# One 64-column matmul in place of two 32-column ones beside two other 32-column matmuls

## The chip, the cores and the metric

The kernel runs on one core of a Trainium2 chip. The metric is device time in microseconds (us), the median of three runs. All times below are of that core.

## The reference

A stack of two transformer layers is followed by a third block with attention, spatial gating, a cross attention and a mixture of experts, all in fp32 on 512 tokens of width 1024. The change touches the mixture of experts alone. Each token is routed to 2 of 16 experts; the reference computes all of them and weighs them:

```python
for e in range(N_EXPERTS):
    he = jax.nn.silu(t @ w_gate[e]) * (t @ w_up[e])
    y = y + combine[:, e:e + 1] * (he @ w_down[e])
```

with t of 512x1024, w_gate and w_up of 1024x512 and w_down of 512x1024 for each expert.

## The kernel before

The kernel sorts the experts by the number of tokens that chose them, and gathers their tokens into tiles of at most 128 rows. A popular expert has a tile to itself. Experts with few tokens share one: `SHARED` names, for a tile, triples (place of the expert in the sorted order, first row, rows). Tile 0 holds two experts of 64 rows each. Tile 1 holds four experts of 32 rows. Tile 2 holds places 6 and 7 with 32 rows each and place 8 with 64 rows, which is written as two parts of 32 rows. `GROUPS` is the order of the tiles: 0, 2, (8 and 10), 7, (9 and 11), 6, 5, 4, 3, 1. For each, `fan` computes the gate and up products (1024 deep, 512 wide, into two PSUM banks), and `fold` the down product (512 deep, 1024 wide). The fan of a tile runs ahead of the fold of the one before it: fan 0, fold 0, fan 2, fan (8, 10), fold 2, fan 7, fold (8, 10), and so on.

For a shared tile the gathered rows are the stationary operand, in plain fp32, and the expert's weights stream from their buffers (`RAW`, and `ST` or `X` where a buffer of another stage is reused) as they come from HBM. Each part of the tile is a matmul of its own: 128 rows deep, as many columns wide as the part has rows, 512 elements streamed, with its output on the PSUM partitions that start at the part's first row. `fan_shared` goes through 8 steps of k for each of gate and up, 16 in all, and `fold_shared` through 4 steps for each of two halves, 8 in all. I call one of these 24 a step; it issues one matmul call for each part (the inner loop over `SHARED[i]`). The profile shows every fp32 call as two MATMUL records, each with a weight load of its own. Other tiles use weights split into two parts (`WH`, `WL`) by ScalarE and VectorE and three matmuls with all 128 columns.

Each weight buffer is 512 KB. SyncE's queue loads them in a fixed order; a load waits until the tile that had its buffer 24 loads before was used (key `wf`, raised by the last matmul that reads it, or `lo`, raised when it was split). Which instruction comes when on each engine is fixed at build time by a planner (`lay_out`) that keeps a clock of its own for each engine. A shared tile's matmul call costs it 856 / (number of parts) ns, so a step costs 856 ns there whatever the number of parts.

GpSimd gathers the rows of a tile (`XG`) and adds a tile's results into `sum` in DRAM by indirect transfers (`sum<-EY,PUT`), one after the other.

Of the kernel before, what the change touches and what calls it, by code (L numbers as in the profile page):

```python
# [343 lines left out]
def build(nc, A, out):  # L344
# [133 lines left out]
    G, S, TP, OP = Ring(ps[0:3]), Ring(ps[3:5]), Ring(ps[5:7]), Ring(ps[7:8])  # L478
# [23 lines left out]
    def view(ap, kind):  # L502
        if kind == "A":
            return ap.rearrange("p (a c) -> p a c", a=4)
        if kind == "B":
            return ap.rearrange("p (a c) -> p a c", a=2)
        return ap.rearrange("p (a s c) -> p a s c", a=2, s=2)
# [7 lines left out]
    def tile_k(w, k, n):  # L515


        if n == 512:
            return w.rearrange("(p k) c -> p k c", k=8)[:, k:k + 2, :], "B"
        return w.rearrange("(p k) (s c) -> p k s c", k=4, s=2)[:, k, :, :], "B"  # L520
# [35 lines left out]
    def cols(T, n=128):  # L556
# [5 lines left out]


    SHARED = {0: ((0, 0, 64), (1, 64, 64)), 1: ((2, 0, 32), (3, 32, 32), (4, 64, 32), (5, 96, 32)),
              2: ((6, 0, 32), (7, 32, 32), (8, 64, 32), (8, 96, 32))}
    PLACES = {i: sorted({p for p, _, _ in parts}) for i, parts in SHARED.items()}
    GROUPS = ((0,), (2,), (8, 10), (7,), (9, 11), (6,), (5,), (4,), (3,), (1,))
    SLOTS = sum(GROUPS, ())
    LAST = SLOTS[-1]
# [6 lines left out]
    def tensor(pe):  # L576
        pe.c = 0

        def tile(src, kind, use="split"):
            c = pe.c  # L580
            pe.c += 1
            if c == len(TILES):
                TILES.append((src, kind, use))
                split = sum(w is not None for w in WAT[MARKS["few"]:]) if "few" in MARKS else None
                WAT.append(None if use == "whole" else c % 8 if split is None else split % 4)
            if use == "whole":
                return c, None, None
            k = kind if kind == "A" else "B"
            return c, view(WH[:, WAT[c], :], k), view(WL[:, WAT[c], :], k)

        def whole_tile(c):
            return view(RAW[RAWSLOT[c] if c < len(RAWSLOT) else 0][:, :], "B")
# [183 lines left out]
        def weight(place, name, k, use):  # L776


            if place < 2:
                return tile(*tile_k(A[name][0, 15 - place], k, 1024 if name == "w_down_2" else 512), use)  # L780
            return tile((name, k, 16 + place if place < 16 else place - 15), "B", use)
# [4 lines left out]
        def fan(gr):  # L786

            if gr[0] in SHARED:
                yield from fan_shared(gr[0])
                return  # L790
            for k in range(8):
                if k % 2 == 0:
                    tiles = [split_weight(gr, name, k) for name in ("w_gate_2", "w_up_2")]
                done = lambda i, c: [("wf", c)] if i == gr[-1] and k % 2 else []
                for i in gr:
                    if small(i):
                        pe.wait_ge(*(yield [("ex", i, 0), *[("raw", c) for c, _, _ in tiles],
                                            G.ask(("fan", i)) if k == 0 else None]))
                        ex, o = pe.slot("ex", i)[1], pe.slot("fan", i)
                        for g, (c, _, _) in enumerate(tiles):  # L800
                            t = pe.mm(o[64 * g:64 * g + 64, :], ex[:, k, 0:64], whole_tile(c)[:, k % 2, :], k == 0, k == 7, 445)
                        keys = done(i, tiles[0][0]) + done(i, tiles[1][0]) + ([("fan", i), ("free", ("ex", i))] if k == 7 else [])
                        if keys:
                            t.then_inc(*pe.sig("pe_gemm", *keys))
                        continue
                    for g, (c, wh, wl) in enumerate(tiles):
                        pe.wait_ge(*(yield [("ex", i, k // 4), ("lo", c), G.ask(("fan", i, g)) if k == 0 else None]))
                        ex, o = pe.slot("ex", i)[0], pe.slot("fan", i, g)
                        pe.mm(o[:, :], ex[:, k, :], wh[:, k % 2, :], k == 0, False)
                        pe.mm(o[:, :], ex[:, k, :], wl[:, k % 2, :], False, False)  # L810
                        t = pe.mm(o[:, :], ex[:, 8 + k, :], wh[:, k % 2, :], False, k == 7)
                        keys = done(i, c) + ([("fan", i, g)] if k == 7 else []) + (
                            [("free", ("ex", i))] if k == 7 and g else [])
                        if keys:
                            t.then_inc(*pe.sig("pe_gemm", *keys))

        def fan_shared(i):

            for k in range(0, 8, 2):
                tiles = [{p: weight(p, name, k, "whole")[0] for p in PLACES[i]} for name in ("w_gate_2", "w_up_2")]  # L820
                for g in range(2):
                    pe.wait_ge(*(yield [("ex", i, k // 4), *[("raw", c) for c in tiles[g].values()],
                                        G.ask(("fan", i, g)) if k == 0 else None]))
                    ex, o = pe.slot("ex", i)[1], pe.slot("fan", i, g)
                    for h in range(2):
                        for p, r, n in SHARED[i]:
                            t = pe.mm(o[r:r + n, :], ex[:, k + h, r:r + n], whole_tile(tiles[g][p])[:, h, :], k + h == 0,
                                      k + h == 7, 856 / len(SHARED[i]))
                            last = r + n == 128 or p != SHARED[i][-1][0]
                            end = k + h == 7 and r + n == 128  # L830
                            keys = ([("wf", tiles[g][p])] if h and last else []) + ([("fan", i, g)] if end else []) + (
                                [("free", ("ex", i))] if end and g else [])
                            if keys:
                                t.then_inc(*pe.sig("pe_gemm", *keys))
# [28 lines left out]

        def fold_shared(i):
            for k in range(4):
                tiles = {p: weight(p, "w_down_2", k, "whole")[0] for p in PLACES[i]}
                for nh in range(2):
                    pe.wait_ge(*(yield [("eh", i), *[("raw", c) for c in tiles.values()],
                                        S.ask(("fold", i, nh)) if k == 0 else None]))
                    eh, o = pe.slot("eh", i)[1], pe.slot("fold", i, nh)  # L870
                    for p, r, n in SHARED[i]:
                        t = pe.mm(o[r:r + n, :], eh[:, k, r:r + n], whole_tile(tiles[p])[:, nh, :], k == 0, k == 3,
                                  856 / len(SHARED[i]))
                        last = r + n == 128 or p != SHARED[i][-1][0]
                        end = k == 3 and r + n == 128
                        keys = ([("wf", tiles[p])] if nh and last else []) + ([("fold", i, nh)] if end else []) + (
                            [("free", ("eh", i))] if end and nh else [])
                        if keys:
                            t.then_inc(*pe.sig("pe_gemm", *keys))
# [2174 lines left out]
    gemms, _, extra = tensor(lister)  # L3054
# [17 lines left out]
    for c, (src, kind, use) in enumerate(TILES):  # L3072
# [49 lines left out]
        i = c - moe  # L3122
# [14 lines left out]
    def strands(lane):  # L3137
        lane.expert, lane.real = None, not isinstance(lane.e, Dry)
        if lane.name == "T":
            _, main, extra = tensor(lane)  # L3140
            return main, extra, []
        return {"A": scalar, "V": vector, "G": pool, "S": sync}[lane.name](lane)
# [5 lines left out]
    parts = {ln.name: strands(ln) for ln in lanes}  # L3148
# [68 lines left out]
```

## Time and profile before

| | |
|---|---|
| time, median of 3 runs | 2116.9 us (2114.93 to 2122.71) |
| profiled execution, its own time | 2114.93 us |
| span in its profile | 2113.1 us |
| TensorE matmul busy | 2012.1 us, 95% |
| VectorE busy | 1264.4 us, 60% |
| ScalarE busy | 983.1 us, 47% |
| bytes moved by DMA | 337.99 MB, mean 160 GB/s |

The page counts the matmuls of parallel column groups as one stretch of busy time, since it takes the union of their records. A record of a matmul includes its way through the array, so it is longer than the distance to the next one; the distances between starts are what to read. The experts' stage covers about the last 300 us of the span. In it the DMA engines are nearly always busy.

### The profile page before, as it was taken

What the parts mean: (1) busy time and instruction counts of PE and PEld (TensorE: products, weight loads), DVE (VectorE), ACT (ScalarE), POOL (GpSimd) and SP (SyncE); (2) the same over time, 40 slices, a digit from 0 to 9 for tenths busy, and PEclk for the clock granted to TensorE, in tenths of its full rate; (3) what the DMA queues carried; (4) which work ended last, traced back from release to release, by engine and by line L of the source; (5) the groups of instructions that cost most, each with busy time, mean ns of one, the idle gap of its engine ahead of it and who ended that gap; (6) DMA issues with size and microseconds to landing.
All of it is one profiled execution on the core that took longest, in us unless ns stands there. A gap on an engine that the chain in (4) does not pass through costs nothing.

```text
span 2113.1 us, 27983 instructions
## 1 busy us (share of the span) xinstructions
PE 2012.1 (95%) x10531; PEld 1595.4 (75%) x10531; DVE 1264.4 (60%) x2204; ACT 983.1 (47%) x1630; POOL 137.0 (6%) x238
## 2 busy tenths in 40 slices
PE   8999999999999999988999999999899999899795
PEld 7877778888888877768888888878778787646462
DVE  5575856585846356665757775737753546536563
ACT  4444545455534355544544553533563234136452
POOL 0000020000001000001000002102000000111101
PEclk9999999999999999999999999999999999999897
DMA  6235244542632333312435262462425526899898
GB/s 209 74 105 156 94 140 138 195 148 88 200 120 80 95 125 122 97 57 101 138 121 179 80 219 70 132 183 81 150 71 164 153 70 229 308 403 375 257 358 313
DMA packets 193854, 337.99 MB, mean 160 GB/s; under 512 B 15878, under 2 KB 103190, under 8 KB 193712
## 3 DMA queue, kind: packets, MB, share of 16 engines
q1 hardware_dynamic: 190096, 327.09, 45.6%
q0 software_dynamic: 3616, 9.03, 1.9%
q8 instruction: 86, 1.41, 0.3%
q14 instruction: 56, 0.46, 0.1%
HBM read 307.12 MB, written 32.51 MB: 161 GB/s over the span
## 4 chain that ended last, share of the span: by engine, by line
PE 77%; DMA 8%; DVE 7%; ACT 3%; POOL 2%; issue 2%; SPq 1%; DVEq 0%; ACTq 0%; POOLq 0%
PE ps L183 72%; PE ps L186 5%; POOL SM L218 2%; DMA ST<-in_w_up_dram 1%; DMA sum<-EY,PUT 1%; DVE WL L198 1%; ACT ST L194 1%; SPq L223 1%; DMA RAW<-in_w_down_dram 1%; DVE X L208 1%; DMA XG<-hd,IDX 1%; POOL SM L215 1%; ACT WH L194 1%; DMA ed<-ST 1%; DMA ONDP<-qkd 1%
## 5 line engine op out<-in xcount | busy, mean ns | idle before, releaser
L198 DVE TENSOR_TENSOR WL<-RAW,WH 128x1024 fp32r<-128x1024 f32 x394 | 475.0, 1221 | 268.3 <-ACT WH L194 265.4
L194 ACT ACTIVATE WH<-RAW 128x1024 fp32r<-128x1024 f32 x394 | 410.5, 1055 | 320.0 <-PE ps L183 192.6
L183 PE MATMUL ps<-XH,WH 128*128 128x512 f32 (+1 forms) x880 | 324.3, 368 | 3.8 <-DVE WL L198 3.8
L183 PE MATMUL ps<-XL,WH 128*128 128x512 f32 (+1 forms) x880 | 321.7, 366 | 0.0
L183 PE MATMUL ps<-XH,WL 128*128 128x512 f32 (+1 forms) x880 | 321.5, 365 | 0.0
L183 PE MATMUL ps<-WH,XH 128*128 128x512 f32 (+1 forms) x736 | 296.8, 403 | 2.5 <-ACT ST L194 2.5
L183 PE MATMUL ps<-WH,HR 128*128 128x512 f32 x928 | 289.2, 390 | 0.0
L183 PE MATMUL ps<-WH,XL 128*128 128x512 f32 (+1 forms) x736 | 284.8, 387 | 0.0
L183 PE MATMUL ps<-WL,XH 128*128 128x512 f32 (+1 forms) x736 | 284.1, 386 | 0.0
L183 PEld LDWEIGHTS ps<-WH,HR 128*128 128x128 f32 x928 | 174.2, 188 | 36.0
L183 PEld LDWEIGHTS ps<-XH,WH 128*128 128x128 f32 x880 | 168.8, 192 | 30.4 <-DVE WL L198 4.6
L183 PEld LDWEIGHTS ps<-XH,WL 128*128 128x128 f32 x880 | 168.5, 192 | 26.0
L183 PEld LDWEIGHTS ps<-XL,WH 128*128 128x128 f32 x880 | 168.7, 192 | 25.4
L183 PE MATMUL ps<-WL,HR 128*128 128x512 f32 x464 | 180.5, 389 | 0.0
L183 PEld LDWEIGHTS ps<-WH,XH 128*128 128x128 f32 x736 | 138.8, 189 | 33.8 <-issue 6.1
L183 PEld LDWEIGHTS ps<-WH,XL 128*128 128x128 f32 x736 | 138.5, 188 | 28.8
L183 PEld LDWEIGHTS ps<-WL,XH 128*128 128x128 f32 x736 | 139.1, 189 | 23.3
L218 POOL TENSOR_TENSOR SM<-SM 128x1 f32<-128x1 f32 (+3 forms) x106 | 68.2, 644 | 820.7 <-DVE SM L1948 441.6
L194 ACT ACTIVATE FR<-ps 128x512 f32<-128x512 f32 x80 | 47.9, 598 | 147.0 <-PE ps L183 146.6
L183 PEld LDWEIGHTS ps<-WL,HR 128*128 128x128 f32 x464 | 87.1, 188 | 17.9
L198 DVE TENSOR_TENSOR HR<-HZ,HR 128x256 fp32r<-128x256 f32 (+1 forms) x92 | 65.8, 735 | 57.3 <-ACT HR L194 56.6
L183 PE MATMUL ps<-WH,EX 128*128 128x512 f32 x224 | 78.2, 410 | 9.7 <-DVE WL L198 9.0
(368 smaller groups left out, 2781.4 us busy)
## 6 DMA issues: line engine op xcount, KB each, us to landing
RAW<-in_ffn_w_dram SPq DMA_DIRECT2D x164, 512.0 KB, 4.5
RAW<-in_w_down_dram SPq DMA_DIRECT2D x63, 512.0 KB, 14.5
RAW<-in_w_gate_dram SPq DMA_DIRECT2D x61, 512.0 KB, 9.6
RAW<-in_w_up_dram SPq DMA_DIRECT2D x57, 512.0 KB, 9.6
RAW<-in_w_in_dram SPq DMA_DIRECT2D x30, 512.0 KB
RAW<-in_ev_w_in_dram SPq DMA_DIRECT2D x20, 512.0 KB
RAW<-in_ple_w_gate_dram SPq DMA_DIRECT2D x16, 512.0 KB
RAW<-in_od_w_in_dram SPq DMA_DIRECT2D x32, 256.0 KB
```

Source lines behind the costliest of these rows:

```text
L183: return self.go(ns).matmul(o, lhsT=l, rhs=x, start=st, stop=sp)
L186: return self.go(110).transpose(o, i, ident)
L194: return self.go(0.83 * n + 55.0 + (130.0 if bias is not None else 0.0) + (100.0 if acc is not None else 0.0)).activation(o, i, f, scale=s ...
L198: return self.go(1.04 * n + 68.0).tensor_tensor(o, a, b, op)
L208: return self.go(1.04 * n + 130.0).scalar_tensor_tensor(out=o, in0=a, scalar=s, in1=b, op0=op0, op1=op1)
L215: return e.tensor_scalar(o, i, s1, None, op0) if op1 is None else e.tensor_scalar(o, i, s1, s2, op0, op1)
L218: return self.go(290.0).tensor_tensor(o, a, b, op)
L223: return e.dma_start(o, i)
```

## The change

Tile 2's third and fourth part, both of expert place 8, become one part of 64 rows. The machinery that let two parts share one weight tile goes away with them: `tiles` is a list with one entry for each part again, and the keys that free a weight tile are raised by the one matmul that reads it last. The same weights are loaded in the same order into the same buffers, and the arithmetic is the same.

```diff
     SHARED = {0: ((0, 0, 64), (1, 64, 64)), 1: ((2, 0, 32), (3, 32, 32), (4, 64, 32), (5, 96, 32)),
-              2: ((6, 0, 32), (7, 32, 32), (8, 64, 32), (8, 96, 32))}
-    PLACES = {i: sorted({p for p, _, _ in parts}) for i, parts in SHARED.items()}
+              2: ((6, 0, 32), (7, 32, 32), (8, 64, 64))}
...
-                tiles = [{p: weight(p, name, k, "whole")[0] for p in PLACES[i]} for name in ("w_gate_2", "w_up_2")]
+                tiles = [[weight(p, name, k, "whole")[0] for p, _, _ in SHARED[i]] for name in ("w_gate_2", "w_up_2")]
...
-                        for p, r, n in SHARED[i]:
-                            t = pe.mm(o[r:r + n, :], ex[:, k + h, r:r + n], whole_tile(tiles[g][p])[:, h, :], k + h == 0,
-                                      k + h == 7, 856 / len(SHARED[i]))
-                            last = r + n == 128 or p != SHARED[i][-1][0]
-                            end = k + h == 7 and r + n == 128
-                            keys = ([("wf", tiles[g][p])] if h and last else []) + ([("fan", i, g)] if end else []) + (
+                        for c, (p, r, n) in zip(tiles[g], SHARED[i]):
+                            t = pe.mm(o[r:r + n, :], ex[:, k + h, r:r + n], whole_tile(c)[:, h, :], k + h == 0, k + h == 7,
+                                      856 / len(SHARED[i]))
+                            end = k + h == 7 and (p, r, n) == SHARED[i][-1]
+                            keys = ([("wf", c)] if h else []) + ([("fan", i, g)] if end else []) + (
```

`fold_shared` is changed in the same way.

## Rows read from the trace of the kernel before

**Rows 1.** The page: span, TensorE's busy time, granted clock and DMA in 40 slices.

```profile
span 2113.1 us, 27983 instructions
...
PE 2012.1 (95%) x10531; PEld 1595.4 (75%) x10531; DVE 1264.4 (60%) x2204; ACT 983.1 (47%) x1630; POOL 137.0 (6%) x238
...
PEclk9999999999999999999999999999999999999897
DMA  6235244542632333312435262462425526899898
```

**Rows 2.** Timeline of PE, end of fold 0 and fan 2: start, length, what.

```profile
1850.79 0.59 PE L183 MATMUL ps<-RAW,EG 128*64 128x512 f32 x1
...
1851.32 2.33 PE L183 MATMUL ps<-X,EF 128*32 128x512 f32 x17
...
1854.36 10.90 PE L183 MATMUL ps<-RAW,EF 128*32 128x512 f32 x99
1865.19 0.50 PE L183 MATMUL ps<-WH,EX 128*128 128x512 f32 x1
```

**Rows 3.** Timeline of PE's weight loads: fold 0 (64 columns), fan 2 (32 columns).

```profile
1847.36 0.14 PEld L183 LDWEIGHTS ps<-RAW,EG 128*64 128x64 f32 x2 [0.29 <-issue]
...
1850.36 0.14 PEld L183 LDWEIGHTS ps<-RAW,EG 128*64 128x64 f32 x1 [0.29 <-issue]
...
1851.32 0.16 PEld L183 LDWEIGHTS ps<-X,EF 128*32 128x32 f32 x8 [0.81 <-issue]
1851.78 0.13 PEld L183 LDWEIGHTS ps<-X,EF 128*32 128x32 f32 x4 [0.30 <-issue]
...
1864.22 0.13 PEld L183 LDWEIGHTS ps<-RAW,EF 128*32 128x32 f32 x4 [0.30 <-issue]
```

**Rows 4.** Timeline of PE in fan (8, 10), from 64 to 128 columns.

```profile
1874.73 0.64 PE L183 MATMUL ps<-RAW,EX 128*64 128x512 f32 x1
...
1875.21 0.59 PE L183 MATMUL ps<-RAW,EX 128*64 128x512 f32 x1
...
1875.74 0.50 PE L183 MATMUL ps<-WH,EX 128*128 128x512 f32 x1
1876.07 0.39 PE L183 MATMUL ps<-WL,EX 128*128 128x512 f32 x1
```

**Rows 5.** Timeline of PE, fold 2 (its first 16 and last 48 records).

```profile
1889.79 1.92 PE L183 MATMUL ps<-RAW,EG 128*32 128x512 f32 x16
...
1892.32 5.36 PE L183 MATMUL ps<-RAW,EG 128*32 128x512 f32 x48
1897.61 0.50 PE L183 MATMUL ps<-WH,EX 128*128 128x512 f32 x1
```

**Rows 6.** Windows of PE: length, busy (records), clock, DMA share, GB/s.

```profile
1851.30:1865.10 13.80, 13.80 (x130) 1.00 1.03 401
1889.80:1897.50 7.70, 7.70 (x69) 1.00 1.03 409
1865.10:1888.70 23.60, 22.51 (x96) 1.00 1.03 400
```

**Rows 7.** Chain of waits: issue and landing of a weight tile of fan (8, 10).

```profile
1851.97 13.99 DMA ST<-in_w_up_dram
```

**Rows 8.** Who waited for whom, SyncE's queue, 1870 to 1930: total, times, longest.

```profile
SPq L223 <- PE ps L183: 6.2, 4, 3.3
```

**Rows 9.** The same from 1930 to 2000.

```profile
SPq L223 <- PE ps L183: 32.8, 7, 13.6
SPq L223 <- DVE WL L198: 22.4, 14, 7.8
```

**Rows 10.** Who waited for whom on PE, from 1959 to the end.

```profile
PE ps L183 <- DMA RAW<-in_w_down_dram: 8.7, 3, 5.5
PE ps L183 <- DMA RAW<-in_w_gate_dram: 3.8, 1, 3.8
...
PE ps L183 <- DMA ST<-in_w_up_dram: 2.8, 1, 2.8
```

More of the change, by code:

```diff
@@ L819, in fan_shared @@
             for k in range(0, 8, 2):
-                tiles = [{p: weight(p, name, k, "whole")[0] for p in PLACES[i]} for name in ("w_gate_2", "w_up_2")]
+                tiles = [[weight(p, name, k, "whole")[0] for p, _, _ in SHARED[i]] for name in ("w_gate_2", "w_up_2")]
                 for g in range(2):
-                    pe.wait_ge(*(yield [("ex", i, k // 4), *[("raw", c) for c in tiles[g].values()],
+                    pe.wait_ge(*(yield [("ex", i, k // 4), *[("raw", c) for c in tiles[g]],
                                         G.ask(("fan", i, g)) if k == 0 else None]))
@@ L865, in fold_shared @@
             for k in range(4):
-                tiles = {p: weight(p, "w_down_2", k, "whole")[0] for p in PLACES[i]}
+                tiles = [weight(p, "w_down_2", k, "whole")[0] for p, _, _ in SHARED[i]]
                 for nh in range(2):
-                    pe.wait_ge(*(yield [("eh", i), *[("raw", c) for c in tiles.values()],
-                                        S.ask(("fold", i, nh)) if k == 0 else None]))
+                    pe.wait_ge(*(yield [("eh", i), *[("raw", c) for c in tiles], S.ask(("fold", i, nh)) if k == 0 else None]))
                     eh, o = pe.slot("eh", i)[1], pe.slot("fold", i, nh)
-                    for p, r, n in SHARED[i]:
-                        t = pe.mm(o[r:r + n, :], eh[:, k, r:r + n], whole_tile(tiles[p])[:, nh, :], k == 0, k == 3,
+                    for c, (p, r, n) in zip(tiles, SHARED[i]):
+                        t = pe.mm(o[r:r + n, :], eh[:, k, r:r + n], whole_tile(c)[:, nh, :], k == 0, k == 3,
                                   856 / len(SHARED[i]))
-                        last = r + n == 128 or p != SHARED[i][-1][0]
-                        end = k == 3 and r + n == 128
-                        keys = ([("wf", tiles[p])] if nh and last else []) + ([("fold", i, nh)] if end else []) + (
+                        end = k == 3 and (p, r, n) == SHARED[i][-1]
+                        keys = ([("wf", c)] if nh else []) + ([("fold", i, nh)] if end else []) + (
                             [("free", ("eh", i))] if end and nh else [])
```

## The prediction

> **What bounds the kernel now.** I read the page first. TensorE is busy for 95% of the span at nearly full granted clock, and the DMA engines reach eight to nine tenths only in the last eight slices, where the experts' weights are loaded [rows 1]. So the stage of the change has two candidates for its limit, and the question is which of them tile 2's matmuls sit on.
>
> Then the timeline of TensorE around tile 2. Fan 2 starts at 1851.32 and the next group's first matmul at 1865.19 [rows 2]; fold 2 runs from 1889.79 to 1897.61, with four transposes in it [rows 5]. In both stretches TensorE is busy without a gap, at clock 1.00, while DMA is at a share of 1.03 and 401 to 409 GB/s [rows 6]. DMA is saturated too, but TensorE does not wait for it there: it runs at its own pace.
>
> What that pace is the weight loads tell. In fan 2 four loads of 32 columns start together, one for each part, and the next four come one round later: from 1851.78 to 1864.22 there are 29 rounds, (1864.22 - 1851.78) / 29 = 0.429 us each [rows 3]. In fold 0, with two parts of 64 columns, a round has two loads and is as long: seven rounds from 1847.36 to 1850.36, 0.429 us [rows 3]. So the parts of a tile run side by side in the array, and a round costs what one matmul costs, however many share it. A step (one call for each part, two records to a call) is two rounds, 0.858 us. Fan 2's 16 steps are 13.7 us, fold 2's 8 are 6.9 us, as the rows show.
>
> **The change part by part.** It removes one of four calls in each of the 24 steps: 48 of 192 matmul records and as many loads. Since a round's length does not depend on the number of calls in it, this removal alone is worth nothing: two parts and four parts both give 0.429. The weight loads (0.13 to 0.14 us) lie beside the streaming, and the transfers, evacuations and semaphores are the same.
>
> What it adds is a round whose parts have unlike widths: 32, 32 and 64 columns. The trace has no such round. It does have what happens when the width changes from one stretch to the next. From the last round with 64 columns (1850.79) to the first with 32 (1851.32) it is 0.53 us, and from there to the second 0.46 (1851.78) [rows 2, 3]. In fan (8, 10), where every step of k goes from 128 columns to 64 and back, the first round of 64 is 0.48 us long (1874.73 to 1875.21), and the next to 128 columns 0.53 (1875.21 to 1875.74) [rows 4]. Two kinds of change of width, and at each the distance is about 0.10 us above the steady 0.429, with a first round behind a change that is 0.03 to 0.05 longer. The pattern of fan (8, 10) repeats in each of the eight steps of k, with everything landed, so it is not the wait for data. I read it as the array finishing what is in it before it takes another width.
>
> If that holds inside a step, the 64-column call can't run beside the 32-column ones. A step becomes: first round of places 6 and 7, second round, change, first round of place 8, second round, change. Its length by the rows is 0.46 + 0.53 + 0.48 + 0.53 = 2.00 us against 0.858, so 1.14 us more. The distance from 32 to 64 columns no row shows; I take the 0.53 of these two. The bounds: with no price for the change itself, four rounds at 0.429 are 1.72 us, 0.86 more; with each change waiting for the whole record of 0.59 us before it and a 0.05 us restart, 0.46 + 0.64 + 0.48 + 0.64 = 2.22, 1.36 more. If unlike widths can run together after all, nothing more.
>
> The Trainium skill, page "TensorEngine Tiling (Array Packing)", section "Tiling Modes", says that changing the tiling mode, not just the tile, drains TensorE; 32 and 64 columns are different modes there. By it a step has two drains, and the sum is the one above. Another page, "TensorE: Matmul & The Clock Gate", Part 3, gives the span of packed matmuls as one matmul plus about 4 ns for each tile, whatever the tiles are; by that a step would stay as it is. The trace agrees with the first where widths change between stretches, and no row mixes them within a round.
>
> Fan 2: 16 x 1.14 = 18.3 us. Fold 2: 8 x 1.14 = 9.1 us. Together 27.4 us of TensorE (bounds 20.6 and 32.6).
>
> **What of it lies on the path.** Three covers are possible.
> First, the stall right behind fan 2: TensorE is idle for 23.60 - 22.51 = 1.1 us up to 1888.7 [rows 6]. The evacuation of the gate bank would find more time ahead of the end of fan 2, since the up half of the last pair of steps gets longer. I take 1.0 us as hidden.
> Second, transfers. A weight tile needed 14 us from issue to landing at 1852 [rows 7], so a backlog of about 14 us / 1.3 us = 11 tiles (512 KB at 401 GB/s are 1.3 us) stood ahead of it. A slower fan 2 frees its 24 tiles in 16 x 2.0 = 32 us, 1.33 us each, which is just what the DMA moves, so DMA goes on nearly without a pause and gains on TensorE. But that lead is worth nothing later: between 1870 and 1930 the load queue waits for TensorE only 6.2 us [rows 8], and TensorE waits for no weights; from 1930 to 2000 the queue waits 32.8 us for TensorE and 22.4 us for the splitting of tiles [rows 9]. So by 1930 the lead is already as long as 24 buffers allow, and from there loads come at the pace at which TensorE frees them. A lead reached earlier is capped at the same 24 buffers.
> Third, the end. There TensorE does wait for weights, 8.7 + 3.8 + 2.8 = 15.3 us [rows 10]. Those are the 48 tiles of tile 1, more than the 24 buffers hold; their loads start only as earlier tiles are used, so they move with TensorE, and the waits stay. I take nothing as hidden here, and 15.3 as the bound.
>
> Sum: 27.4 - 1.0 = 26.4 us. On the profiled execution's 2114.9 that is 2141.3; the median of the runs shown lies 2.0 us above it, so 2143.
>
> Behind the step everything shifts as one: gathers and scatters on GpSimd wait for TensorE or for evacuations. The planner sees 856 ns for a step as before; only the release of a weight tile within a step moves in its clock, by at most 856/3 - 856/4 = 71 ns for the first part and 143 for the second. I expect its orders to stay.
>
> **The rivals.**
> Unlike widths run side by side (not slower). The place is the first step of fan 2, and it decides whether the third matmul starts some 10 ns behind the second or 0.5 us behind. For it: parts of equal width overlap fully. Against: the 0.53 us at every change of width. Price: 24 x 0 = 0, so 2117.
> The added time is hidden by the weights at the end. For it: 15.3 us of waits for transfers there, and DMA at a share near 1 for most of the stage. Against: the queue's waits for TensorE before it. 27.4 - 1.0 - 15.3 = 11.1, so 2128.
> The three calls run wholly one after the other, places 6 and 7 too, because the pairs aren't formed when a drain is pending: six rounds of 0.429 and 0.24 for the two changes, 2.81 us, 1.96 more, times 24 is 47 us, so 2163. For it: no row shows a pair followed by an unlike call. Against: calls of equal width always pair in this trace.
> The planner's 71 to 143 ns turn an order on some queue, and a scatter or a load moves: some 9 us either way on top of the sum, about 2134 or 2152.
>
> **How the numbers follow.** The forecast, with 2136 to 2149 around it (its bounds 0.86 and 1.36 for a step, less 1.0), has 0.62. Side by side 0.10; hidden at the end 0.13; all in sequence 0.07; an order that turns 0.06, half of it below the forecast; what I haven't seen, faster by over 0.5%, 0.02. The range from 2124 to 2158 takes in the forecast, the hidden case and the turned orders, 0.81. About 0.5%, 10.6 us, is what a measurement of this kernel tells from no change, so "same" ends at 2127.5: side by side and a good third of the hidden case, 0.15. Slower is 0.83.
>
> **What the profile after would show.** In the timeline of fan 2, pairs of 32-column records, then single 64-column records, with about 2.0 us from step to step, and fan 2 some 32 us long instead of 13.9. Fold 2 some 16 us in place of 6.9 of matmuls. 144 records for tile 2 in place of 192. The wait behind fan 2 gone. From fan 7 on, each landmark later by about 26 us, and the same waits for weights at the end. If the 64-column records start with the 32-column ones, the first step falls; if fan 2 is longer but tile 1's waits shrink from 15.3 us, the second does. A granted clock below 1.00 in fan 2, which I don't expect since the array goes on streaming for 1.7 of 2.0 us, would add to it.

## The result and the profile after

The changed kernel takes 2140.97 us (median of 4 runs, 2137.71 to 2146.26) against 2115.91 us (4 runs, 2113.06 to 2122.71) before: ratio 1.0121, 95% interval 1.0094 to 1.0149, so 25 us slower (20 to 32). The forecast was 2143, with 2124 to 2158 around it. The profiled execution took 2139.27 us, 24.3 more than that of before.

The page of the changed kernel, lines as in [rows 1]:

```profile
span 2137.4 us, 27887 instructions
...
PE 2037.3 (95%) x10483; PEld 1597.0 (75%) x10483; DVE 1265.6 (59%) x2204; ACT 984.1 (46%) x1630; POOL 135.6 (6%) x238
...
PEclk9999999999999999999999999999999999999898
DMA  6235244642532324313426343444235256987897
```

TensorE has 48 matmul records fewer and 25.2 us more busy time, as much as the whole loss; its clock is what it was. The share of 95% has not moved and shows nothing of it.

The weight loads at the start of fan 2, from PE's timeline of the changed kernel, to be held against [rows 3]:

```profile
1850.85 0.14 PEld L183 LDWEIGHTS ps<-X,EF 128*32 128x32 f32 x4 [0.81 <-issue]
1851.83 0.19 PEld L183 LDWEIGHTS ps<-X,EF 128*64 128x64 f32 x2 [0.84 <-issue]
1852.83 0.11 PEld L183 LDWEIGHTS ps<-X,EF 128*32 128x32 f32 x1 [0.81 <-issue]
...
1853.82 0.19 PEld L183 LDWEIGHTS ps<-RAW,EF 128*64 128x64 f32 x2 [0.84 <-issue]
```

Before, a step's loads came in two bunches, 0.43 us apart. Now the 32-column loads stand alone, the 64-column ones follow 0.98 us later, and the next step begins 1.98 us after this one (1850.85 to 1852.83). Nothing of the wide call lies beside the narrow ones.

PE's timeline of the changed kernel at the landmarks of [rows 2, 5]:

```profile
1848.87 4.59 PE L183 MATMUL ps<-X,EF 128*32 128x512 f32 x13
...
1880.62 0.50 PE L183 MATMUL ps<-WH,EX 128*128 128x512 f32 x1
...
1902.84 1.16 PE L186 MATMUL ps<-ident,XG 128*128 128x128 f32 x8
1903.93 4.04 PE L183 MATMUL ps<-RAW,EG 128*32 128x512 f32 x12
...
1908.57 11.98 PE L183 MATMUL ps<-RAW,EG 128*32 128x512 f32 x36
1920.48 0.50 PE L183 MATMUL ps<-WH,EX 128*128 128x512 f32 x1
```

Fan 2 began at 1848.87 here and at 1851.32 before, 2.45 us earlier; the stages ahead of the change vary by some microseconds from run to run (fan 2 starts between 1842.8 and 1854.4 in the traces of this document). From there to the first matmul of (8, 10) it is 31.75 us in place of 13.87. The transposes ahead of fold 2 stand at 1902.84 in place of 1888.70, and fan 7 starts at 1920.48 in place of 1897.61: that stretch has grown from 8.91 to 17.64 us.

Windows of PE in the changed kernel (length, busy, clock, DMA share, GB/s), against [rows 6]:

```profile
1848.80:1880.60 31.80, 31.80 (x98) 1.00 1.00 378
1903.90:1921.00 17.10, 17.10 (x55) 1.00 0.93 329
1880.60:1902.80 22.20, 22.20 (x93) 1.00 0.72 261
```

While fan 2 runs, the DMA engines stay full. In the group behind it they drop to 0.72, and the load queue waits for TensorE for 19.3 us of it (1880 to 1903) where it waited 3.3 us before (1865 to 1889): the loads are there already as far ahead as the 24 buffers allow. The idle time of TensorE in that window (1.1 us before) is gone.

Who waited for whom in the changed kernel: on PE from 1850 to the end, then SyncE's queue from 1895 to 1955 and from 1955 to 2025, against [rows 8 to 10]:

```profile
PE ps L183 <- DMA RAW<-in_w_down_dram: 11.9, 4, 5.6
...
PE ps L183 <- DMA RAW<-in_w_gate_dram: 3.0, 1, 3.0
PE ps L183 <- DMA ST<-in_w_up_dram: 1.8, 1, 1.8
```

```profile
SPq L223 <- PE ps L183: 37.4, 12, 4.9
...
SPq L223 <- PE ps L183: 31.5, 7, 12.7
SPq L223 <- DVE WL L198: 23.1, 14, 8.6
```

The load queue now waits for TensorE where it hardly did before, and later as it did before. The waits for weights at the end are 11.9 + 3.0 + 1.8 = 16.7 us in place of 15.3.

### The profile page after: what moved, and what is told of

The parts are those of the page before. It is cut to its first block, busy times and chain, and to the rows that moved or that the text cites. A ratio compares the mean times of both kernels' runs of the same rounds, so it can differ in the third digit from the quotient of the medians.

```text
span 2137.4 us, 27887 instructions
## 1 busy us (share of the span) xinstructions
PE 2037.3 (95%) x10483; PEld 1597.0 (75%) x10483; DVE 1265.6 (59%) x2204; ACT 984.1 (46%) x1630; POOL 135.6 (6%) x238
## 4 chain that ended last, share of the span: by engine, by line
PE 78%; DMA 8%; DVE 6%; ACT 3%; POOL 2%; issue 2%; SPq 1%; DVEq 0%; POOLq 0%; ACTq 0%
PE ps L183 73%; PE ps L186 5%; POOL SM L218 2%; DVE WL L198 1%; DMA sum<-EY,PUT 1%; SPq L223 1%; ACT ST L194 1%; DMA RAW<-in_w_down_dram 1%; DMA ONDP<-qkd 1%; DMA XG<-hd,IDX 1%; POOL SM L215 1%; DVE X L208 1%; ACT WH L194 1%; DMA NQ<-qqd 0%; DMA qkd<-ST 0%
## 5 line engine op out<-in xcount | busy, mean ns | idle before, releaser
L183 PEld LDWEIGHTS ps<-XL,WH 128*128 128x128 f32 x880 | 168.4, 191 | 25.2
L183 PEld LDWEIGHTS ps<-WL,HR 128*128 128x128 f32 x464 | 87.1, 188 | 17.9
```

The costliest lines, as they stand in the source:

```text
L183: return self.go(ns).matmul(o, lhsT=l, rhs=x, start=st, stop=sp)
```

## The experiments

All ratios are to the kernel before on the same chip, with 95% intervals. Its median there was 2113.88 us for the first four rows, 2115.02 for the next four and 2115.36 for the last two, so medians of different groups compare to 1 or 2 us at best. The diffs below are cut to the lines that make the experiment; lines that only keep the keys or the planner's cost of a call are left out. In the traces of all experiments but the last three, ScalarE, VectorE, GpSimd and SyncE take their work in the order of the kernel before.

| kernel | median, us | ratio | interval |
|---|---|---|---|
| wide call in fan 2 only | 2131.86 | 1.0091 | 1.0071 to 1.0111 |
| wide call in fold 2 only | 2121.37 | 1.0037 | 1.0023 to 1.0051 |
| wide call first, at partition 0 | 2143.00 | 1.0142 | 1.0122 to 1.0162 |
| three calls of 32 | 2114.17 | 0.9999 | 0.9978 to 1.0019 |
| changed kernel, fan 2 grouped by width | 2138.09 | 1.0097 | 1.0059 to 1.0136 |
| tile 0 as four calls of 32 | 2115.76 | 0.9989 | 0.9961 to 1.0018 |
| tile 1 mixed in place of tile 2 | 2118.41 | 1.0008 | 0.9986 to 1.0030 |
| two steps of k together, fans and folds | 2106.66 | 0.9963 | 0.9939 to 0.9986 |
| the same in the fans only | 2099.81 | 0.9919 | 0.9894 to 0.9944 |
| the same in the folds only | 2110.33 | 0.9980 | 0.9960 to 1.0000 |

### The change in two halves

```diff
+    MIXED = {**SHARED, 2: ((6, 0, 32), (7, 32, 32), (8, 64, 64))}
...
-                        for p, r, n in SHARED[i]:
+                        for p, r, n in MIXED[i]:
```

in `fan_shared` alone, and in `fold_shared` alone.

> The kernel before with the 64-column call in fan 2 alone; fold 2 keeps four calls of 32 columns. Theory (a change of width inside a step makes the array finish first, and nothing behind fan 2 hides it): a step of fan 2 takes 1.98 us as in the changed kernel, fan 2 31.8 us in place of 13.9, the stall of 1.1 us behind it goes, and the time rises by 16 to 17 us. Fold 2 keeps rounds of 0.429 us. Rival (the two halves are not additive, because a later wait takes up what is below some size): the time rises by less than 10 us although fan 2 is 17.9 us longer.

> The kernel before with the 64-column call in fold 2 alone; the planner's clock is kept as before by a cost in proportion to the columns. Theory: 8 steps at 1.98 us in place of 0.86, fold 2 longer by 8.7 to 9 us and the time up by the same, since the next waits stand where they did. Rival (hidden by the waits at 1960 to 2000 or at the end): the time rises by less than 3 us.

The fan alone made the kernel slower by 19 us (15 to 23), the fold alone by 8 us (5 to 11). In the first trace fan 2 runs from 1845.86 to 1877.62, 31.76 us, and fold 2 is as before; in the second fan 2 is 13.87 us (1847.92 to 1861.79) and the fold reads, in PE's timeline:

```profile
1885.08 4.04 PE L183 MATMUL ps<-RAW,EG 128*32 128x512 f32 x12
...
1889.73 11.98 PE L183 MATMUL ps<-RAW,EG 128*32 128x512 f32 x36
1901.64 0.50 PE L183 MATMUL ps<-WH,EX 128*128 128x512 f32 x1
```

16.6 us from the first of its matmuls to the next group, as in the changed kernel and not 7.8 as in [rows 5]. The halves add up, and neither is hidden: both rivals, under 10 and under 3 us, fall outside the intervals.

### Place or width

```diff
-              2: ((6, 0, 32), (7, 32, 32), (8, 64, 64))}
+              2: ((8, 0, 64), (6, 64, 32), (7, 96, 32))}
```

> The changed kernel with the 64-column call first, on PSUM partitions 0 to 63, and the two 32-column calls on 64 to 95 and 96 to 127; the same loads, but the experts of tile 2 meet the wrong rows, so that part of the output is not the reference's. Theory (unlike widths can't be in the array together, wherever they stand): a step is 1.98 us again, and the time equals the changed kernel's within 3 us, about 25 us above the kernel before. Rival (it is the place: a 64-column call that starts at partition 64 behind 32-column calls is what cannot run beside them): the three run side by side, a step is 0.86 us and the time is that of the kernel before.

The ratio is 1.0142 where the changed kernel has 1.0121, the same within the intervals. The loads of its fan 2:

```profile
1853.19 0.19 PEld L183 LDWEIGHTS ps<-RAW,EF 128*64 128x64 f32 x2 [0.84 <-issue]
1854.19 0.11 PEld L183 LDWEIGHTS ps<-X,EF 128*32 128x32 f32 x1 [0.81 <-issue]
...
1855.17 0.19 PEld L183 LDWEIGHTS ps<-RAW,EF 128*64 128x64 f32 x2 [0.84 <-issue]
```

Again 1.98 us a step, wide call first. So neither the place nor the order in the step matters.

### Number or width

```diff
-              2: ((6, 0, 32), (7, 32, 32), (8, 64, 32), (8, 96, 32))}
+              2: ((6, 0, 32), (7, 32, 32), (8, 64, 32))}
```

> The kernel before with three calls of 32 columns in a step of tile 2, the fourth left out: rows 96 to 127 of the tile are not computed, all loads stay. Theory: three equal widths still run side by side, a round is 0.429 us, fan 2 13.9 us, the time within 2 us of the kernel before. Rival (it is the number: three calls, or an odd number, break the pairing of the rounds): a step of 1.3 us or more, and the time up by 10 us or more.

No difference (0.9999). Three loads in a bunch, 0.42 to 0.43 us apart, to the end of fan 2:

```profile
1855.32 0.12 PEld L183 LDWEIGHTS ps<-RAW,EF 128*32 128x32 f32 x3 [0.31 <-issue]
1855.74 0.12 PEld L183 LDWEIGHTS ps<-RAW,EF 128*32 128x32 f32 x3 [0.31 <-issue]
```

Fan 2 is 13.87 us long (1842.84 to 1856.71), to the hundredth what it is with four calls. Three calls of one width share a round as four do; the changed kernel has three calls too. The fewer calls gave nothing, as predicted.

### Rounds alone, and the price of a change of width

In the changed kernel's fan 2, four narrow calls and then two wide ones:

```diff
-                    for h in range(2):
-                        for p, r, n in SHARED[i]:
+                    for wide in (False, True):
+                        for h, (p, r, n) in [(h, x) for h in range(2) for x in SHARED[i] if (x[2] > 32) == wide]:
```

> The changed kernel with the calls of fan 2 in another order: within each group of two steps (h = 0 and 1) first the four 32-column calls, then the two 64-column calls. Fold 2 as in the changed kernel. Theory: half the changes of width in fan 2. A change there and back costs 1.985 - 4 x 0.429 = 0.27 us beside the rounds, so two steps take 8 x 0.429 + 0.27 = 3.70 us in place of 3.97, fan 2 29.6 us in place of 31.8, and the time is 2.2 us below the changed kernel's. The larger part, that the 64-column rounds run alone, stays. Rival (what costs is only the restart at each change, and calls without a change between them overlap): two steps take 1.7 + 0.3 us, fan 2 about 16 us, the time 16 us below the changed kernel's.

```profile
1849.11 0.14 PEld L183 LDWEIGHTS ps<-X,EF 128*32 128x32 f32 x4 [0.81 <-issue]
...
1850.95 0.19 PEld L183 LDWEIGHTS ps<-X,EF 128*64 128x64 f32 x2 [0.84 <-issue]
...
1852.82 0.11 PEld L183 LDWEIGHTS ps<-X,EF 128*32 128x32 f32 x1 [0.81 <-issue]
```

Two steps take 3.71 us, and fan 2 is 29.61 us long (1849.12 to 1878.73), 2.14 less than in the changed kernel, where 2.2 was expected. In the time, a ratio of 1.0097 against 1.0121, the difference is within the intervals of the two, so it is the trace that shows it. That divides the added 1.13 us of a step: 0.86 because the wide call's two rounds stand alone, 0.27 for the two changes.

### Many calls of one width

Tile 0's `((0, 0, 64), (1, 64, 64))` as `((0, 0, 32), (0, 32, 32), (1, 64, 32), (1, 96, 32))`:

> The kernel before with tile 0's two parts of 64 columns cut into four of 32, two for each expert. Theory (a round costs the same whatever equal widths share it, so the number of calls is free): rounds of 0.429 us in fan 0 and fold 0, no change of width between fold 0 and fan 2, the time within 1 us of the kernel before. Rival (twice the weight loads and calls cost issue time): rounds longer than 0.43 us and the time up by 2 us or more.

0.9989, no difference. The end of fold 0 and the start of fan 2:

```profile
1853.57 0.12 PEld L183 LDWEIGHTS ps<-RAW,EG 128*32 128x32 f32 x2 [0.30 <-issue]
...
1854.00 0.13 PEld L183 LDWEIGHTS ps<-X,EF 128*32 128x32 f32 x4 [0.30 <-issue]
```

Another buffer, another bank, another wait, but the same width, and the distance is 0.43; in [rows 2] it was 0.53 at the same place, where 64 columns gave way to 32. That takes away the last other reading of the 0.53, that it was the wait of a new tile.

### The same cost where the weights set the pace

Tile 1, the last, gets the mixed step; the wide call uses the weights of its two experts in turn:

```diff
+    MIXED = {**SHARED, 1: ((2, 0, 32), (3, 32, 32), (4, 64, 64))}
...
-                        for p, r, n in SHARED[i]:
+                        for p, r, n, q in [(*x, 5 if (i, x[0], h) == (1, 4, 1) else x[0]) for x in MIXED[i]]:
```

> The kernel before with tile 1, the last one, mixed instead of tile 2: calls of 32, 32 and 64 columns, the wide one streaming expert place 4's weights in even steps and place 5's in odd ones, so that all 48 loads are still read and freed. Rows of places 4 and 5 get wrong values. TensorE has the same 24 steps at 1.98 in place of 0.86 us, 27 us more. Theory (here TensorE waits 15.3 us for weights that arrive at the rate of the DMA, so a part is hidden): fan 1 is about 32 us long in place of 19 with its waits, the waits for w_gate and w_up vanish, the last w_down tile lands within 5 us of where it did, and the time rises by 6 to 14 us. Rival (the loads are freed later too, so the waits stay as they did with tile 2): the time rises by 25 us or more.

The time rose by 1.7 us (-3 to 6), where 6 to 14 was expected. Windows from the start of fan 1 to its end and on to the end of fold 1 (length, busy of PE, PEld, DVE, ACT, POOL, then clock, DMA share, GB/s), first with tile 1 mixed, then before:

```profile
2044.00:2076.60 32.60, 31.88 (x97) 5.36 (x96) 0.77 (x3) 5.21 (x7) 1.56 (x1) 1.00 0.99 354
2076.60:2100.00 23.40, 22.64 (x77) 7.65 (x77) 5.14 (x5) 2.05 (x3) 1.56 (x1) 1.00 0.89 320
```

```profile
2045.60:2069.30 23.70, 16.28 (x129) 4.21 (x128) 0.74 (x3) 4.06 (x6) 1.56 (x1) 0.86 0.99 354
2069.30:2094.80 25.50, 16.06 (x92) 7.04 (x92) 5.14 (x6) 3.62 (x5) 1.55 (x1) 0.87 1.03 392
```

And the load queue's timeline, last tiles of the mixed tile 1:

```profile
2057.19 19.86 SPq L223 DMA_DIRECT2D RAW<-in_w_down_dram  x20
```

The w_down loads are issued from 2057.19, before from 2056.90, while fan 1 began at 2044.04 here and at 2045.62 before: counted from there they are 1.9 us later, little beside the 9 us by which fan 1 has grown.

TensorE's idle time in the two windows falls from 49.2 - 32.3 = 16.9 to 56.0 - 54.5 = 1.5 us, 15.4 less: the waits for weights are gone. Its busy time rises by 22.2 us, not by 24 x 1.13 = 27.1, because the clock is 1.00 in place of 0.86 and 0.87. Before, two stretches in these windows ran at the lower level (1.2 GHz), the second of them from within a wait of 5.5 us for w_down: the 16 records behind that wait took 3.64 us, the 16 before it 1.92. With the waits gone, both windows run at 2.4 GHz.

That leaves 22.2 - 15.4 = 6.8 us more in these two profiles. From the start of fan 1 to the end it is 74.2 us here and 67.5 before, but 67.7 to 69.6 in the six experiments on tiles 0 and 2, which have the same matmuls there as the kernel before; so the profile of before is at the low end, and the cost in the traces is 4.6 to 6.7 us. The same edit costs 25 us at tile 2 and 6 us at most, by the interval, at tile 1.

### A version that is faster than both

If each change of width costs, the groups (8, 10) and (9, 11) pay it in every step of k [rows 4]. Two steps together halve that:

```diff
-            for k in range(8):
-                if k % 2 == 0:
-                    tiles = [split_weight(gr, name, k) for name in ("w_gate_2", "w_up_2")]
+            for k0 in range(0, 8, 2):
+                tiles = [split_weight(gr, name, k0) for name in ("w_gate_2", "w_up_2")]
...
-                for i in gr:
+                for i, k in [(i, k0 + d) for i in gr for d in range(2)]:
```

and the same in `fold`.

> The kernel before, with the calls of the groups (8, 10) and (9, 11) in another order: for two steps of k at a time first the 128-column matmuls of the large tile, then the 64-column ones of the small tile. That halves the 24 changes from 128 to 64 columns and back; each there and back costs 0.10 + 0.05 + 0.10 + 0.10 = 0.35 us in the trace before. Theory: 12 x 0.35 = 4.2 us less TensorE time, and the time 3 to 4 us lower. Rival (a later wait takes it up, or ScalarE's and VectorE's splits are not ready in time): within 1 us of the kernel before.

The time fell by 8 us (3 to 13). Two steps of k, in PE's timeline:

```profile
1868.82 0.50 PE L183 MATMUL ps<-WH,EX 128*128 128x512 f32 x1
...
1873.63 0.50 PE L183 MATMUL ps<-WH,EX 128*128 128x512 f32 x1
```

4.81 us, where the kernel before needs twice 2.60 (1873.14 to 1875.74): 0.39 less for each change there and back, so 12 x 0.39 = 4.7 us. That lies within the interval but below the 8 us, so the halves were run apart:

> The kernel before with the two-step order in the fans of (8, 10) and (9, 11) alone. In the run with both, two steps of k took 4.81 us in place of 5.20, 0.39 us for each change there and back that went. Theory (the gain is those changes): 8 x 0.39 = 3.1 us, 2113 less 3 in a profile and 0.15% in the ratio. Rival (about half of the 8 us that both together gave comes from orders on ScalarE and VectorE that the planner turned, and from where a stall falls): this run gives 6 us or more although only 8 changes go.

> The kernel before with the two-step order in the folds of (8, 10) and (9, 11) alone. Theory (the gain is those changes): 4 x 0.39 = 1.6 us, less than 0.1%, not told from no change. Rival (the rest of the gain of both together lies here: the 3.1 us in which TensorE waited for the copy of EG ahead of fold (9, 11), and the chain of scatters behind it): 4 us or more.

The folds alone gave 0.20% (0 to 0.40), 4 us, with 1.6 expected; the interval holds both. The fans alone gave 17 us (12 to 22) though only 8 changes went, 3.1 us. Here the theory's size fails and the rival holds: most of this gain is not width. PE's waits in that run, from 1840 on:

```profile
PE ps L183 <- DVE WL L198: 4.0, 2, 3.7
```

Before it was 9.4 us for the same row, and the 3.1 us for `EG` (the transposes ahead of fold (9, 11) behind VectorE's copy) are gone altogether. Together with the changes of width that is 3.1 + 3.1 + 5.4 = 11.6 us; from the start of fan 2 to the end the profile has 250.9 us in place of 261.8. The planner turned some orders on ScalarE and VectorE in this kernel, most of them between 1950 and 1976, where the evacuations into `EX` come earlier than before. It turned the same ones in the kernel with fans and folds, where TensorE waited 8.5 us for `WL`. That the turned orders moved the stalls is therefore likely and not shown, since no run turned them alone; why the run with fans and folds gained less stays open too.

## Why the prediction was right

**The rounds.** The prediction held that parts of equal width share a round and that the call removed is worth nothing. Three calls of 32 (0.9999, fan 2 13.87 us as before) and tile 0 in four parts (0.9989) show it.

**The change of width.** It took 2.00 us for a step, from distances at changes between stretches; the trace has 1.98 (0.45, 0.53, 0.48, 0.52 in every step of fan 2). The distance from 32 to 64 columns, which no row showed, is 0.53 like the others. The prediction read these distances as the array finishing what is in it; the runs show the distances and that unlike widths take turns, not what the array does meanwhile, and the next width starts 0.06 us ahead of the end of a record of 0.59. The Trainium skill's rule that a change of the tiling mode drains TensorE ("TensorEngine Tiling (Array Packing)", Tiling Modes) agrees with this trace inside a step too, by these 0.52 and 0.53 us. The span of packed matmuls that the Trainium skill gives ("TensorE: Matmul & The Clock Gate", Part 3), one matmul and about 4 ns for each further tile, fits equal widths in these runs, where three or four records side by side end within 0.60 to 0.62 us and one takes 0.59; it does not fit the mixed step of 1.98 us, and the page's table has packings of one tile size only.

**The terms.** Fan 2: 18.3 forecast, 17.9 measured (31.75 - 13.87). Fold 2: 9.1 forecast, 8.7 measured (17.64 - 8.91). Hidden behind fan 2: 1.0 forecast, 1.3 measured (1865.19 to 1888.70 is 23.51 us, 1880.62 to 1902.84 is 22.22). Sum 25.3 where 26.4 was forecast, and at the start of fan 7 the changed kernel is later by 25.3 - 2.45 = 22.9 us, which is 1920.48 - 1897.61. The end comes 24.3 later, 1.4 more. The waits for weights are 1.4 us longer, but the agreement proves nothing: from the start of fan 7 to the end, with the same matmuls in the same order, it is 215.5 us in the profile of before, 216.9 in that of the changed kernel and 216.7 to 220.2 in the six experiments on tiles 0 and 2. So the sum in TensorE's time is confirmed, and that the medians differ by 25.06, within 1.4 of the forecast's 26.4, is in part luck.

**The cover.** The lead in weights was said to be worth nothing, since 24 buffers cap it anyway. The DMA share of 0.72 behind fan 2, the queue's 37.4 us of waits for TensorE, and 16.7 us of waits at the end bear that out. The argument holds for time added ahead of tile 1 and no further: time added inside tile 1 does use the waits up, as the mixed tile 1 showed. I read this as the question whether the time is added before or after the loads for the waiting tiles are issued; two places were tried, and the rule is argued from them.

**The rivals.** Side by side, all in sequence (a step of 2.81) and hidden at the end are each contradicted by the trace. The planner turned no order: with the lines aligned, the instruction lists of ScalarE, VectorE, GpSimd and SyncE are the same in both kernels.

## What to carry to other kernels

In these runs matmuls in different column groups of the array share their time only while all are equally wide (fp32, 32 and 64 columns); when the parts of a tile are unlike, cut the wide ones down to the narrow width, since up to four calls in a round cost what two do. Where wide and narrow matmuls must alternate, group them, as each change there and back costs 0.27 us (32 and 64 columns) to 0.39 us (64 and 128). Before pricing added TensorE time, ask where the loads that it waits for later are issued: here time added ahead of that point moved the wait, and time added behind it filled the wait.

## What was not expected

The same 27 us of TensorE work cost 25 us at one tile and 1.7 us (-3 to 6) at another, more cover than the 15.3 us of waits in the trace: some 5 us of it are the stretches at 1.2 GHz, which went with the waits. And reordering the calls of two groups, meant to save 3.1 us, gave 17 (2099.81 us, the fastest kernel here): the stalls in the stretch from 1960 to 2000 changed while ScalarE and VectorE had the same work in a slightly different order, which is the likely cause and was not tested alone.
